# Three output tiles in each step of an entry, and squares summed by four column groups of TensorE

## The reference

```python
def second_block(x, p, ...):
    h = x
    for i in range(DEPTH_2):                     # 2 layers
        g = norm_gains[i]
        f = swiglu(rmsnorm(h, g[0]), ffn_gate[i, 0], ffn_up[i, 0], ffn_down[i, 0])
        h = h + MACARON * rmsnorm(f, g[1])
        mix = hybrid_mixer(rmsnorm(h, g[2]), ...)
        h = h + rmsnorm(mix, g[3])
        f = swiglu(rmsnorm(h, g[4]), ffn_gate[i, 1], ffn_up[i, 1], ffn_down[i, 1])
        h = h + MACARON * rmsnorm(f, g[5])
        gate = jax.nn.sigmoid(rmsnorm(h, g[6]) @ w_ple_gate[i])
        h = h + rmsnorm((p[i] @ w_ple[i]) * gate, g[7])
    return h
```

## Time and profile before

| | |
|---|---|
| median of 3 runs | 3004.22 us (3003.27 to 3006.89) |
| profiled execution | 3005.28 us |
| its span, first to last instruction | 3003.5 us |
| PE busy (matmuls) | 2862.1 us, 95% |
| PE weight loads | 2384.8 us, 79% |
| DVE busy | 1558.5 us, 52% |
| ACT busy | 1145.5 us, 38% |
| POOL busy | 243.3 us, 8% |
| mean granted clock of PE | 0.98 |
| window attention of the first block | about 274 to 373 us |
| first entry (feed-forward, layer 0) | from 804 us |
| other entries begin at | 1175, 1445, 1834, 1896, 2272, 2542, 2932 us |

### The profile page before, as it was taken

The page is one execution under the profiler, slowest core; times in us unless marked ns, Lnnn a source line. Parts: engine busy times, 40 slices in busy tenths (PEclk is TensorE's granted clock), DMA queues, the critical chain, the costliest instruction groups (busy, mean ns, idle before and its releaser), DMA issues.

```text
span 3003.5 us, 42576 instructions
## 1 busy us (share of the span) xinstructions
PE 2862.1 (95%) x17236; PEld 2384.8 (79%) x17236; DVE 1558.5 (52%) x2618; ACT 1145.5 (38%) x1861; POOL 243.3 (8%) x272
## 2 busy tenths in 40 slices
PE   6999889899999999999999999899999999999997
PEld 3866888778788888777888888788888778888886
DVE  5744465544354434855644436644436755644346
ACT  3333444243333323455433224532324564333234
POOL 0000065400000000200000000000000201000000
PEclk7999999999999999999999999999999999999998
DMA  6222000022232332301222332233332301332321
GB/s 237 64 67 73 3 8 3 15 91 92 77 106 98 98 106 92 117 32 50 72 97 98 99 106 78 77 98 99 98 105 96 95 29 43 98 98 93 104 91 57
DMA packets 69778, 244.92 MB, mean 82 GB/s; under 512 B 8464, under 2 KB 10640, under 8 KB 68944
## 3 DMA queue, kind: packets, MB, share of 16 engines
q1 hardware_dynamic: 69584, 242.21, 24.5%
HBM read 234.70 MB, written 3.15 MB: 79 GB/s over the span
## 4 chain that ended last, share of the span: by engine, by line
PE 67%; DVE 3%; ACT 2%; issue 1%; DVEq 0%; ACTq 0%
PE pair L228 20%; PE pair L230 20%; PE pair L229 20%; PE pair L2568 2%; PE pair L2597 2%; PE pair L357 2%; PE pair L2607 1%; ACT w_hi_at L182 1%; DVE rstd_at L473 1%; DVE work_at L308 0%; DVE w_lo_at L190 0%; PE pair L491 0%; DVE residual L314 0%; DVE h_lo_at L319 0%; PE pair L488 0%
## 5 line engine op out<-in xcount | busy, mean ns | idle before, releaser
L228 PE MATMUL pair<-h_hi_at,w_hi_at 128*128 128x512 f32 (+1 forms) x2048 | 781.3, 381 | 35.9 <-DVE h_lo_at L319 31.4
L229 PE MATMUL pair<-h_lo_at,w_hi_at 128*128 128x512 f32 (+1 forms) x2048 | 759.1, 371 | 0.0
L230 PE MATMUL pair<-h_hi_at,w_lo_at 128*128 128x512 f32 (+1 forms) x2048 | 759.0, 371 | 0.0
L190 DVE TENSOR_TENSOR w_lo_at<-w_raw,w_hi_at 128x1024 fp32r<-128x1024 f32 x348 | 439.4, 1263 | 430.6 <-ACT w_hi_at L182 430.4
L182 ACT ACTIVATE w_hi_at<-w_raw 128x1024 fp32r<-128x1024 f32 x348 | 364.8, 1052 | 523.5 <-PE pair L230 512.1
L228 PEld LDWEIGHTS pair<-h_hi_at,w_hi_at 128*128 128x128 f32 x2048 | 389.0, 190 | 112.2 <-DVE h_lo_at L319 37.4
L229 PEld LDWEIGHTS pair<-h_lo_at,w_hi_at 128*128 128x128 f32 x2048 | 389.1, 190 | 67.1 <-issue 0.5
L230 PEld LDWEIGHTS pair<-h_hi_at,w_lo_at 128*128 128x128 f32 x2048 | 388.9, 190 | 65.3
L2330 DVE TENSOR_TENSOR work_at<-pair,rstd_at 128x512 f32<-128x512 f32 (+1 forms) x184 | 122.1, 667 | 363.2 <-PE pair L230 363.1
L228 PE MATMUL pair<-a_hi_at,w_hi_at 128*128 128x512 f32 (+1 forms) x792 | 290.1, 366 | 0.0
L229 PE MATMUL pair<-a_lo_at,w_hi_at 128*128 128x512 f32 (+1 forms) x792 | 289.4, 365 | 0.0
(11 more groups left out here) (423 smaller groups left out, 3975.8 us busy)
## 6 DMA issues: line engine op xcount, KB each, us to landing
w_raw<-in_weights SPq DMA_DIRECT2D x431, 512.0 KB, 3.4
residual<-in_x SPq DMA_DIRECT2D x1, 2048.0 KB, 12.0
cos_sin_at<-rope_table SPq DMA_DIRECT2D x2, 1024.0 KB, 4.8
by_sin_at<-delta_at SPq DMA_DIRECT2D x32, 64.0 KB, 2.0
by_sin_at<-kd_at SPq DMA_DIRECT2D x32, 64.0 KB, 2.0
out<-residual SPq DMA_DIRECT2D x16, 128.0 KB, 1.7
q_wide<-in_ctx SPq DMA_DIRECT2D x1, 1024.0 KB, 12.9
rope_table<-zb SPq DMA_DIRECT2D x1, 1024.0 KB, 4.2
```

Source lines behind the costliest of these rows:

```text
L190: eng.tensor_tensor(self.w_lo[:, g % self.split].rearrange("p k n -> p (k n)"), self.w_raw[:, g % RAW], self.w_hi[:, g % self.split].rearr ...
L228: pe.matmul(out, sh, mh, start=start, stop=False)
L229: pe.matmul(out, sh, ml, start=False, stop=False)
L230: return pe.matmul(out, sl, mh, start=False, stop=stop)
```

## The change

- `Entry` multiplies three output tiles in each of its 16 steps (banks 0, 1 and 7, both halves in one bank). This holds for feed-forwards and mixers. The PLE keeps two. With `BEHIND = 0` the third product follows the first two.
- The squares of four tiles are summed by one call of `pe_sums`: four f32 products with 32 columns of ones each, which write to the partitions 0 to 31, 32 to 63, 64 to 95 and 96 to 127 of the bank. After two batches of a half, ACT copies these partial sums (`act_partial`) and one product with the full matrix of ones adds the four groups (`pe_fold`); the root's scale is divided by 32. The squares of tile t are taken behind the rounding of tile t + 1.
- The third granule is split inside the entry (ACT behind the third rounding, DVE in step 3), the fourth where the third was; behind the entry ACT and DVE run one granule further ahead in their loops.
- The mixer's ring of banks and the feed-forward's banks are dealt out anew, with waits for older tiles; in the feed-forward's last tile two waits go. The mixer's exit makes both first-half squares wait for the last first half, and its first sum stands in the second half of tile 6 and no longer in that of tile 7.
- The windowed attention scores two blocks of keys with one product of 256 columns where two lie side by side: 80 products for 144.

```diff
-    FIRST_BANKS = ((0, 1), (6, 7))
+    FIRST_BANKS = (0, 1, 7)
+    BEHIND = 0
...
-    def act_tile(self, act, half, t):
+    def act_round(self, act, half, t):
         x, c, n = self.kit.residual, cols(half), half * KD + t
         if self.leave:
             act.wait_ge(*self.added(n + 1))
         act.activation(self.hi[:, t, c], x[:, t, c], ACT.Copy, scale=self.gain(t)).then_inc(self.rounded.sem, 1)
+
+    def act_square(self, act, half, t):
+        n = half * KD + t
         if n >= 4:
-            act.wait_ge(*self.summed(n - 3))
-        act.activation(self.sq[:, n % 4], x[:, t, c], ACT.Square).then_inc(self.squared.sem, 1)
+            act.wait_ge(*self.summed(n // 4))
+        act.activation(self.sq[:, n % 4], self.kit.residual[:, t, cols(half)], ACT.Square).then_inc(self.squared.sem, 1)
...
+    def act_partial(self, act, half):
+        act.wait_ge(*self.summed(2 * half + 2))
+        act.activation(self.partial[:, cols(half)], self.kit.banks[self.SUM_BANK[half]][:, 0:HALF],
+                       ACT.Copy).then_inc(self.part_copied.sem, 1)
 
     def act_root(self, act, half):
...
+        act.wait_ge(*self.folded(half + 1))
+        act.activation(self.kit.rstd[:, cols(half)], self.kit.banks[self.SUM_BANK[half]][:, HALF:], ACT.Sqrt,
+                       scale=1.0 / (32 * D), bias=self.kit.eps[:, 0:1]).then_inc(self.rooted.sem, 1)
...
+    def pe_sums(self, pe, batch):
+
+        half, second = divmod(batch, 2)
+        pe.wait_ge(*self.squared(4 * batch + 4))
+        for q in range(4):
+            last = pe.matmul(self.kit.banks[self.SUM_BANK[half]][32 * q:32 * q + 32, 0:HALF], self.kit.square("ones")[:, 0:32],
+                             self.sq[:, q], start=not second, stop=bool(second), skip_group_check=True)
+        last.then_inc(self.summed.sem, 1)
+
+    def pe_fold(self, pe, half):
+        pe.wait_ge(*self.part_copied(half + 1))
+        pe.matmul(self.kit.banks[self.SUM_BANK[half]][:, HALF:], self.kit.square("ones"), self.partial[:, cols(half)],
+                  start=True, stop=True).then_inc(self.folded.sem, 1)
+
+    def pe_product(self, pe, n, m):
+
+        kit, (half, t) = self.kit, divmod(n, KD)
+        c = cols(half)
+        if m == 0:
+            pe.wait_ge(*self.h_ready(n + 1))
+        if n == 0:
+            pe.wait_ge(kit.w_split, self.g0 + m + 1)
+        last = matmul3(pe, kit.banks[self.FIRST_BANKS[m]][:, c], kit.w_tile(self.g0 + m, t),
+                       (self.hi[:, t, c], self.lo[:, t, c]), t == 0, t == KD - 1)
+        if n == 2 * KD - 1:
+            last.then_inc(kit.w_used, 1)
...
+        for n in range(2 * KD):
+            if n in (4, 8, 12):
+                self.pe_sums(pe, n // 4 - 1)
+            for m in range(2):
+                self.pe_product(pe, n, m)
+            if self.leave and n == 1:
+                self.leave.pe_sum(pe, 1)
+            if n >= self.BEHIND:
+                self.pe_product(pe, n - self.BEHIND, 2)
+            if n == 10:
+                self.pe_fold(pe, 0)
+        self.pe_sums(pe, 3)
+        for n in range(2 * KD - self.BEHIND, 2 * KD):
+            self.pe_product(pe, n, 2)
...
             for t in range(KD):
-                self.act_tile(act, half, t)
+                self.act_round(act, half, t)
                 if half == 0 and t == 1 and leave:
                     leave.act_late(act)
+                if half == 0 and t == 2:
+                    kit.w_make_hi(act, self.g0 + 2)
                 if half == 0 and t == 3 and leave:
                     leave.act_squares(act, 1)
                 if half == 0 and t == 4:
                     if leave:
                         leave.act_root(act, 1)
-                    kit.w_make_hi(act, self.g0 + 2)
+                    kit.w_make_hi(act, self.g0 + 3)
                 if half == 1 and t == 1:
+                    self.act_partial(act, 0)
+                if half == 1 and t == 3:
                     self.act_root(act, 0)
+                if t >= 1:
+                    self.act_square(act, half, t - 1)
+            self.act_square(act, half, KD - 1)
+        self.act_partial(act, 1)
...
-        makes = {KD: lambda: kit.w_make_lo(dve, self.g0 + 2)}
+        makes = {3: lambda: kit.w_make_lo(dve, self.g0 + 2), KD: lambda: kit.w_make_lo(dve, self.g0 + 3)}
...
-                            window = [(ka[:, b * P:(b + 1) * P], va[:, b, lane]) for b in range(lo_b, hi_b)]
-                            context = [(ka[:, b * P:(b + 1) * P], va[:, b, lane]) for b in (4, 5)]
-
+                            window, context = list(range(lo_b, hi_b)), [4, 5]
                             blocks, at = (window + context, 3) if n == 0 else (context + window, 0)
+                            pieces = [(ka[:, b * P:(b + len(blocks[j:j + 2])) * P], j * P)
+                                      for j, b in enumerate(blocks) if j % 2 == 0]
...
@@ class Ffn
-    BANKS = ((0, 1), (3, 2))
+    BANKS = ((0, 1), (7, 4), (3, 6))
+    DOWN_BANKS = (5, 7, 4, 2)
...
-            if f >= 2:
-                pe.wait_ge(*self.gate_scaled(f - 1))
-                pe.wait_ge(*self.up_scaled(f - 1))
-            for which in range(2):
+            if f >= 3:
+                pe.wait_ge(*self.gate_scaled(f - 2))
+                pe.wait_ge(*self.up_scaled(f - 2))
+            for which in range(f == 1, 2):
...
+                    if f == 1 and k == 1:
+                        self.entry.pe_fold(pe, 1)
...
-            kit.w_make_hi(act, g0 + 2 * f + 3)
+            kit.w_make_hi(act, g0 + 2 * f + 4)
             if f:
                 round_up(f - 1)
             act.wait_ge(*self.gate_scaled(f + 1))
...
-            kit.w_make_hi(act, g0 + 2 * f + 4)
+            if f < FT - 1:
+                kit.w_make_hi(act, g0 + 2 * f + 5)
...
@@ class Mixer
-    RING = (3, 2, 0, 1, 6, 7)
+    RING = (0, 1, 7, 3, 2, 0, 1, 6, 7, 3, 2, 0)
...
-            kit.w_used, self.o0 + t + 1) if half else self.half_done(t - self.full + 1)) for t in (KD - 2, KD - 1)])
+            kit.w_used, self.o0 + t + 1) if half else self.half_done(2)) for t in (KD - 2, KD - 1)])
...
+                if t == 3 and k == 1:
+                    self.entry.pe_fold(pe, 1)
...
-                    if half == 1 and t == KD - 1 and k == 1:
+                    if half == 1 and t == KD - 2 and k == 2:
                         self.exit.pe_sum(pe, 0)
...
         for t in range(self.TILES):
-            kit.w_make_hi(act, g0 + t + 3)
+            if t < self.TILES - 1:
+                kit.w_make_hi(act, g0 + t + 4)
             if t == 3:
...
-            kit.w_make_lo(dve, g0 + t + 3)
             if t == 0:
-                self.entry.dve_rstd(dve)
+                self.entry.dve_rstd(dve, 0)
+                kit.w_make_lo(dve, g0 + 4)
+                self.entry.dve_rstd(dve, 1)
+                dve.wait_ge(*self.entry.rstd_ready(2))
...
+            if 0 < t < self.TILES - 1:
+                kit.w_make_lo(dve, g0 + t + 4)
...
@@ class Ple
-            if t >= 1:
-                self.entry.pe_sum(pe, 0, t - 1)
+            if t == 5:
+                self.entry.pe_sums(pe, 0)
...
+        for n in range(2 * KD):
+            for m in range(2):
+                self.entry.pe_product(pe, n, m)
+            if n == 0:
+                self.entry.pe_sums(pe, 1)
+            if n == KD + 2:
+                self.entry.pe_fold(pe, 0)
+            if n == KD + 4:
+                self.entry.pe_sums(pe, 2)
+        self.entry.pe_sums(pe, 3)
...
+                if t == 2 and k == 2:
+                    self.entry.pe_fold(pe, 1)
```

More of the change, by code:

```diff
@@ L348, in dve_rstd @@
-    def dve_rstd(self, dve):
-        for half in range(2):
-            dve.wait_ge(*self.rooted(half + 1))
-            dve.reciprocal(self.kit.rstd[:, cols(half)], self.kit.rstd[:, cols(half)]).then_inc(self.rstd_ready.sem, 1)
-        dve.wait_ge(*self.rstd_ready(2))
-    def pe_sum(self, pe, half, t):
-        n = half * KD + t
-        pe.wait_ge(*self.squared(n + 1))
-        pe.matmul(self.kit.banks[self.SUM_BANK[half]][:, 0:HALF], self.kit.square("ones"), self.sq[:, n % 4], start=(t == 0),
-                  stop=(t == KD - 1), skip_group_check=True).then_inc(self.summed.sem, 1)
@@ L360, in pe_products @@
-    def pe_products(self, pe, half, t):
-        kit, c = self.kit, cols(half)
-        pe.wait_ge(*self.h_ready(half * KD + t + 1))
-        for m in range(2):
-            if half == 0 and t == 0:
-                pe.wait_ge(kit.w_split, self.g0 + m + 1)
-            last = matmul3(pe, kit.banks[self.FIRST_BANKS[half][m]][:, 0:HALF], kit.w_tile(self.g0 + m, t),
-                           (self.hi[:, t, c], self.lo[:, t, c]), t == 0, t == KD - 1)
-            if half == 1 and t == KD - 1:
-                last.then_inc(kit.w_used, 1)
@@ L2840, in dve @@
                    b["kd"][:, t - 8])
[L2841 to L2843 removed]
+            dve.tensor_tensor(dst, self.bank(t), kit.rstd[:, :], ALU.mult).then_inc(self.drained.sem, 1)
+            if 0 < t < self.TILES - 1:
```

(2 more changed lines are left out.)

111 lines of the change are left out of this document (49 added, 62 removed).

## The result

The changed kernel takes 3011.04 us (median of 15 runs, 3004.88 to 3016.34), the kernel before 3005.97 beside it (15 runs, 3002.56 to 3008.63). The ratio is 1.0018, 95% interval 1.0011 to 1.0025: about 5 us slower. The profiled execution took 3009.87 us, its span is 3008.1.

What follows compares the result with a forecast made beforehand. PE is busy nearly throughout, so its issue sets the time. Terms -3.0 - 0.6 + 4.6 - 8.2 + 4.4 + 1.9 give -0.9 us: 3004.4 profiled, 3003.3 median, no change; 8 in 10 range 2986 to 3019.

Steps and rivals of the forecast that it cites:

- Batch of sums: In the entries, four tiles' sums need five passes' time, 1.07 us, plus 0.2 for changes of shape: 1.27 us.
- rival B: In the entries, all four column groups run at once: a batch 0.63 us, 15.4 us less, 2988; chance 0.22.
- Entries of mixers and feed-forwards: PE bound from the seventh tile: mixer entries end 1.0 us earlier; second feed-forwards' work ends 4.5 earlier.
- First feed-forward, layer 0: Same working as the mixer's entry, without DVE's adds: wins 0.6 us.
- Tile 6: Behind each mixer's entry, latent roots queue behind a granule waiting for tile 5; PE has nothing for 2.5 us.
- Fold and reciprocal: Each mixer: the other fold gives 0.43 us back, and PE waits 0.45 for the second reciprocal.
- Second feed-forwards: Exit's first sum and DVE's chain come 2.6 us earlier, most of DVE's stand goes: -4.1 us each, -8.2 in two.
- PLE: Root waits for nine products and the fold, exit 2.5 us later; entry itself ends 0.2 earlier: +2.2 each.
- Window attention: 64 pairs of 128-column score pieces at 0.48 us become one of 256 at 0.43: -3.0 us.
- First feed-forward, layer 1: Table load and sigmoids delay the third granule, DVE stands 3.5 us; with fold and half clock: +1.9 us.
- E: Clock rival: waits for third-tile weights thin PE's work in six entries, more at 1.2 GHz: some 9 us, 3012; chance 0.07.

Runs made afterwards that it cites:

- experiment 7: Changed kernel, each batch followed by a second set of four products, single window blocks; only its trace read: four groups 0.45 us, one group 1.82 to the next product.
- experiment 1: Changed kernel with the two latent roots ahead of granule 9's rounding in the mixer's ACT loop: ratio 1.0003 to the kernel before.
- Experiments 2 to 4: Changed kernel, each with one PLE edit: first batch two tiles earlier, ratio 1.0009; folds earlier, 1.0008; sums by tile without folds, 0.9994.
- Experiment 5: Changed kernel with sums by tile, no column groups or folds, in all eight entries, third output tile kept: ratio 1.0063.
- experiments 9 and 11: Third granule later: on the changed kernel with latent roots ahead and PLE sums by tile, 2981.61 us; alone on the changed kernel, 2995.82 us.

## Why the forecast missed

Forecast -0.9 us, measured +4.7 between the traces and about +5 by the medians. That the two are only 6 us apart is luck. At the measured price of a batch the prediction's own sum comes out 12 us lower (24 x 0.51), and costs of 18 us that it did not have came on top. By its own steps:

*Batch of sums*: the term mis-sized. It charged 1.27 us and a batch took 0.76. The step that failed is the reading of the earlier trace rows as "issue in order: a tile's second pass waits for its first", which gave four tiles five passes' time. Those rows have two tiles (`blocks` takes the upper and the under one in turn). Their passes start in pairs 0.01 us apart and 0.06 from pair to pair (400.09, 400.15 and so on), about what one pass alone needs (0.053). A factor of two is all that two tiles can give: the rows showed full overlap. Products in four column groups run side by side in both passes as well (experiment 7). The Trainium skill, TensorE: Matmul & The Clock Gate, Measured speedup vs the span model, gives 2.38 for three column tiles; here four give 3.8 (1.72 to 0.45), and 2.3 with the changes of shape (1.71 to 0.76). The estimate from it under rival B, near 0.7 us a batch, came close to 0.76 with a smaller overlap and no changes of shape in it. The Trainium skill, TensorEngine Tiling (Array Packing), Key Properties, says that a change of tiling mode drains TensorE. Here both changes together cost some 0.3 us; I had charged 0.2.

*Entries of mixers and feed-forwards*: right in sum, for errors that cancel. The mixers' entries were to end 1.0 us earlier and ended 0.9 and 1.5 earlier. The three batches on the path cost 1.5 us less than assumed. What took that back, in layer 1 at full clock: the seventh tile comes 12.3 us behind the entry's start where the forecast had 11.95, in part since DVE wins back 0.75 of its old stand and not 0.92, and PE waits 0.50 for the squares of a later batch, which was not in the sum. In layer 0 the seventh tile comes at 12.9, since the exit's second sum, late behind PE's wait for the third granule, then ran at half clock. I had followed the granule through the queues of ACT and DVE and left out PE's own.

*First feed-forward, layer 0*: -0.6 forecast, -1.8 measured. The cheaper batches (1.5) less PE's wait for the squares (0.5) make the difference within 0.2.

*Tile 6*: right in mechanism and size (2.5 forecast, 2.41 measured, shown by experiment 1). *Fold and reciprocal*: 0.43 and 0.45 forecast, 0.99 together. The term left out of both mixers is the clock. In layer 1 it fell after the stall, 1.5 us. The other 1.9 us in layer 0's mixer lie in the dilated heads, where PE takes 54.9 us from the first to the last product that reads `kd`, and 53.0 in layer 1 and in both layers of the kernel before. What decides is where a stretch at half clock falls. In the kernel before it lies 22.5 to 25.9 us behind the first of these products and costs nothing; in the changed kernel it lies 28.3 to 31.8 behind and costs 1.9. The 14 traces agree. The heads take at most 53.3 us where there is no half clock or one stretch of 3.4 us that begins at most 23 behind the first product, and 54.4 to 54.9 where half clock reaches beyond 27. Why it falls at one place or the other is open.

*Second feed-forwards*: -4.1 each forecast, -3.4 and -4.9 measured. The exit's earlier sum is right (its reciprocal starts 2.5 us earlier, 2.6 forecast); the entry in it is right by the same errors that cancel.

*PLE*: the mechanism was right for the tail (fold behind nine products: 2.4 forecast, exit's sum 2.3 us later counted from the first 512-column product, 36.48 against 34.18). The step that failed is "the entry itself ends 0.2 earlier". Counted from the embedding's start it ends 1.6 and 2.6 us later, since ACT needs a slot for every square and all four come free at once; the batch then stands where PE reaches it late. And the fold that ACT waits for was counted only at the second root, not at the first. Experiments 2 to 4 show all three. In each PLE the clock is at half for 3.4 us more than before, which is worth 1.5 by the two PLEs of the kernel before (56.0 with such a stretch, 54.5 without).

*Window attention*: -3.0 forecast, -0.9 measured. The step that failed is 0.48 for a pair of pieces against 0.43 for the wide one, from 1.2 us for ten passes. The passes start 0.11 us apart, so a pair is 0.45 and the wide product 0.43: 0.02 x 64 = 1.3 us, and the measured 0.9 is near that. The stretch ahead of the first entry as a whole got 1.5 shorter; what the other 0.6 is no run tells.

*First feed-forward, layer 1*: +1.9 forecast, +0.8 measured. DVE stood 3.1 us for the granule (3.5 forecast), and the clock stayed at half for longer, but the cheaper batches paid for most.

Of the rivals, B was right on the batch and wrong on the total. Experiment 5 shows that the batches did give 20 us, all on the path, to a kernel which without them stands at 1.0063: the third tile, with its early granule, the stalls and the clock, costs that much first. E was right in kind: summed from the granted clock of both traces, PE is at half speed for 14 us more than before in entries, exits and PLEs, and 3.4 more in layer 1's mixer. That its 3012 lies next to the measured 3011 is luck, since it was worked out with batches at 1.27.

## What to carry to other kernels

When a piece of work is moved ahead in hand-ordered queues, follow it on every engine that waits for it, and list what stands behind that wait there. Here VectorE stood 1.1 us, TensorE 1.4, and a small sum for somebody else was queued behind TensorE's wait. That sum held VectorE's reciprocal by 0.2 us at full clock, and by more where the clock had fallen; a later place for the granule gave 14 us. Batching work that hands back slots saves time on the engine that does it and turns a smooth producer into one that stands for the whole batch; either place the batch where the last of its inputs is ready, or leave that stage unbatched. A cheaper operation pays only beside other work that fills its engine: the same batches were worth 20 us with a third tile and nothing with two.

## What the runs showed of the hardware that I had not expected

Four f32 products of 256 columns in four column groups take 0.45 us together, as long as a single full sum (0.43), and 1.72 one after the other in one group. Scoring 256 columns in one product or in two of 128 takes the same time within 0.02 us. In the changed kernel PE waits 1.4 us for the third granule near the start of four entries, with shorter waits around it. In three of them the granted clock was 0.50 (1.2 GHz) for 3.4 us, beginning 0.3 to 2.3 us behind that wait; in the fourth, layer 1's mixer, it stayed at 1.00. With the wait gone (experiments 9 and 11) the clock stayed at 2.4 GHz in all four (1.00 over 24.9 us).
